# The order of small products, sums and table operations in the routing of a mixture of experts, and of its first weight load

## The reference, cut

```python
g_logits = (u @ w_group).astype(jnp.float32) + b_group          # 4 groups
p_grp, g_sel = lax.top_k(softmax(g_logits), 1)
e_logits = (u @ w_router + b_router).reshape(n, N_GROUPS, EXP_PER_GROUP)
...                                                              # the logits of the chosen group
p_exp, e_sel = lax.top_k(softmax(in_grp), TOP_E)                 # 2 experts of 8
gate = p_grp * p_exp / jnp.sum(p_exp, axis=-1, keepdims=True)
expert = g_sel * EXP_PER_GROUP + e_sel                           # 32 experts in all
...                                                              # per expert: silu(x w1) * (x w3), then w2
```

## Time and profile before

| | |
|---|---|
| median of 3 runs | 1541.97 us (1540.78 to 1544.36) |
| the profiled execution | 1542.55 us, span in the trace 1540.7 us |
| busy | PE 1386.6, DVE 719.4, ACT 527.4, POOL 211.2 us |
| transfers | 360.05 MB, mean 234 GB/s over the span |
| chain that ended last | PE 70%, DMA 18%, DVE 3%, ACT 3% |
| TensorE's granted clock, mean | 0.946 of full speed |

### The profile page before, as it was taken

The page is one execution under the profiler, slowest core; times in us unless marked ns, Lnnn a source line. Parts: engine busy times, 40 slices in busy tenths (PEclk is TensorE's granted clock), DMA queues, the critical chain, the costliest instruction groups (busy, mean ns, idle before and its releaser), DMA issues.

```text
span 1540.7 us, 27632 instructions
## 1 busy us (share of the span) xinstructions
PE 1386.6 (90%) x11864; PEld 1168.6 (76%) x11864; DVE 719.4 (47%) x1207; ACT 527.4 (34%) x815; POOL 211.2 (14%) x180
## 2 busy tenths in 40 slices
PE   6999899996777777686999989999999999999997
PEld 6998568764344444344978979999999876899997
DVE  5365665421111121113865664565456564565644
ACT  6346553110000010013334454434435434544342
POOL 4132002200000000000100023211234200111132
PEclk9999999799888798779999999999999999999999
DMA  9341218989999999999635142444454321445340
GB/s 355 139 159 54 85 56 349 393 374 428 428 429 428 428 427 429 428 428 424 238 125 208 66 178 110 163 166 150 148 199 174 141 106 60 159 176 208 126 176 28
DMA packets 32856, 360.05 MB, mean 234 GB/s; under 512 B 5376, under 2 KB 8448, under 8 KB 10752
## 3 DMA queue, kind: packets, MB, share of 16 engines
q1 hardware_dynamic: 32768, 358.76, 58.0%
HBM read 357.70 MB, written 1.05 MB: 233 GB/s over the span
## 4 chain that ended last, share of the span: by engine, by line
PE 70%; DMA 18%; DVE 3%; ACT 3%; issue 2%; SPq 1%; POOL 1%; DVEq 0%; ACTq 0%; POOLq 0%
PE PS L550 42%; DMA expert_w<-in_w 16%; PE PS L563 5%; PE PS L1013 4%; PE PS L603 3%; PE PS L1034 2%; DMA raw_x<-in_ret_qk 2%; PE PS L977 1%; SPq L400 1%; PE PS L1104 1%; PE PS L851 1%; PE PS L1189 1%; ACT wh L1443 1%; PE PS L587 1%; PE PS L579 1%
## 5 line engine op out<-in xcount | busy, mean ns | idle before, releaser
L1961 DVE TENSOR_TENSOR wl<-raw,wh 128x4096 fp32r<-128x4096 f32 (+2 forms) x66 | 267.6, 4054 | 206.8 <-ACT wh L1443 206.7
L1443 ACT ACTIVATE wh<-raw 128x4096 fp32r<-128x4096 f32 (+2 forms) x66 | 219.5, 3326 | 113.8 <-PE PS L550 108.4
L550 PE MATMUL PS<-UH,wh 128*128 128x272 f32 (+1 forms) x840 | 244.5, 291 | 11.9 <-DVE wl L2017 11.6
L550 PE MATMUL PS<-UH,wl 128*128 128x272 f32 (+1 forms) x840 | 241.4, 287 | 0.0
L550 PE MATMUL PS<-UL,wh 128*128 128x272 f32 (+1 forms) x840 | 240.9, 287 | 0.0
L1013 PE MATMUL PS<-expert_w,XW 128*32 128x256 f32 x2048 | 156.5, 461 | 86.7 <-DMA expert_w<-in_w 86.4
L1013 PEld LDWEIGHTS PS<-expert_w,XW 128*32 128x32 f32 x2048 | 70.8, 128 | 161.0 <-DMA expert_w<-in_w 106.9
L550 PEld LDWEIGHTS PS<-UH,wh 128*128 128x128 f32 x840 | 158.9, 189 | 12.9 <-DVE wl L2017 11.6
L550 PEld LDWEIGHTS PS<-UL,wh 128*128 128x128 f32 x840 | 159.3, 190 | 0.4
L550 PEld LDWEIGHTS PS<-UH,wl 128*128 128x128 f32 x840 | 159.1, 189 | 0.0
L2326 DVE TENSOR_TENSOR SG<-PS,SG 128x128 f32<-128x128 f32 x32 | 9.3, 292 | 270.0 <-ACT SG L1712 269.9
(11 more groups left out here) (526 smaller groups left out, 3025.7 us busy)
## 6 DMA issues: line engine op xcount, KB each, us to landing
expert_w<-in_w SPq DMA_DIRECT2D x96, 2048.0 KB, 20.4
raw<-in_up SPq DMA_DIRECT2D x22, 2048.0 KB, 8.2
raw<-in_down SPq DMA_DIRECT2D x16, 1408.0 KB, 6.1
raw<-in_ret_v SPq DMA_DIRECT2D x4, 2048.0 KB, 8.5
raw<-in_ret_gate SPq DMA_DIRECT2D x4, 2048.0 KB, 8.2
raw<-in_ret_o SPq DMA_DIRECT2D x4, 2048.0 KB, 8.6
raw<-in_ret_qk SPq DMA_DIRECT2D x3, 2048.0 KB, 12.9
raw<-in_w_in_ga SPq DMA_DIRECT2D x2, 2048.0 KB, 8.2
```

Source lines behind the costliest of these rows:

```text
L550: mm = pe.matmul(gbank(g)[:, c0:T], w[:, c:c + P], x(k)[:, c0:], start=(k == 0 and j == 0), stop=(k == nk - 1 and j == 2))
L1443: act.activation(WH[n % 2][:, 0:w], raw(n)[:, 0:w], ACT.Copy).then_inc(hi_done, 1)
L1961: dve.tensor_tensor(wl_of(n)[:, 0:w], raw(n)[:, 0:w], WH[n % 2][:, 0:w].bitcast(F32), ALU.subtract).then_inc(lo_done, 1)
```

## The change

Of TensorE's stream: the zero products of banks 0 and 1 move from ahead of the sums to behind them; the keep_busy counts 2, 1, 3 and 10 become 5, none, none and 4; the table's product (L967) moves behind dispatch, and the wait for the table and the load of the loop bound to behind the first hidden products. Of VectorE's: the slots are made from two terms, of which the first (the slot without overflow) and the overflow masks are formed once the ranks are there, without the prefix sums; three operations of the table move behind `window(0)`. Of ScalarE's: the wait for the table moves to its loop bound. Of SyncE's: the load of w2[1] goes ahead of the wait for `wo` and of the eight small tables.

```diff
+            sp.wait_ge(lo_done, 12)
+            load(XPT[2][:], a["w2"][1], xp_full[2])
             sp.wait_ge(unit_done, UNIT0["wo"])
             for name in ("RB", "DESC", "utri", "THR", "IOTA", "WRT", "EBASE", "SLOT"):
                 load(small[name][:], a["m_" + name], moe_in)
-            sp.wait_ge(lo_done, 12)
-            load(XPT[2][:], a["w2"][1], xp_full[2])
...
-            zeroed(0)
-            zeroed(1)
             MM, CC, CB, TA = (small[x] for x in ("MM", "CC", "CB", "TA"))
-            keep_busy(sbank(0), 2)
+            keep_busy(sbank(0), 5)
             pe.wait_ge(rt_m, 1)
...
             mm.then_inc(rank_done, 1)
-            keep_busy(sbank(0), 1)
             pe.wait_ge(rt_m, 2)
...
-            keep_busy(sbank(0), 3)
-            pe.wait_ge(rt_m, 3)
-            pe.matmul(sbank(2)[0:1, 0:OVER + 1], ones[0:NE, 0:1], TA[0:NE, 0:OVER + 1], start=True, stop=True)\
-                .then_inc(rank_done, 1)
+            zeroed(0)
+            zeroed(1)
...
-            keep_busy(sbank(0), 10)
+            keep_busy(sbank(0), 4)
             pe.wait_ge(perm_done, 2)
             pe.wait_ge(rank_free, 1)
             dispatch(True)
+            pe.wait_ge(rt_m, 3)
+            pe.matmul(sbank(2)[0:1, 0:OVER + 1], ones[0:NE, 0:1], TA[0:NE, 0:OVER + 1], start=True, stop=True)\
+                .then_inc(rank_done, 1)
...
-            pe.wait_ge(tbl_done, 1)
...
-            last = pe.value_load(TBL[0:1, ITEMS + 1:ITEMS + 2], min_val=NE - 2, max_val=ITEMS - 2)
             pe.wait_ge(xw_half, 1)
             hidden(0, 0, True)
+            pe.wait_ge(tbl_done, 1)
+            last = pe.value_load(TBL[0:1, ITEMS + 1:ITEMS + 2], min_val=NE - 2, max_val=ITEMS - 2)
             hidden(0, 1)
...
-            act.wait_ge(tbl_done, 1)
             act.nop().then_inc(xye_done, 2)
...
+            act.wait_ge(tbl_done, 1)
             last = act.value_load(TBL[0:1, ITEMS + 1:ITEMS + 2], min_val=NE - 2, max_val=ITEMS - 2)
...
-            dve.wait_ge(rank_done, 3)
-            link(dve.tensor_copy(CC[e, 2:3], sbank(1)[e, NE:NE + 1]))
-            link(dve.tensor_scalar(TA[e, 0:OVER], IO[e, 0:OVER], CC[e, 2:3], None, ALU.is_ge))
-            dve.tensor_copy(TA[e, OVER:OVER + 1], CC[e, 1:2]).then_inc(rt_m, 1)
-            link(dve.tensor_tensor(q["BK"][:], sbank(1)[:, 0:NE], EBASE[:, 1, :], ALU.add))
-            link(dve.scalar_tensor_tensor(out=CODE[:], in0=rank, scalar=float(WIN), in1=bc(q["BK"][:].unsqueeze(1), [P, NT, NE]),
-                                          op0=ALU.is_ge, op1=ALU.mult))
-            link(dve.tensor_tensor(CODE[:], CODE[:], bc(EBASE[:, 0, :].unsqueeze(1), [P, NT, NE]), ALU.add))
-            dve.tensor_tensor(CODE[:], CODE[:], rank, ALU.add).then_inc(rank_free, 1)
+            dve.wait_ge(rank_done, 2)
+            dve.tensor_tensor(CODE[:], rank, bc(EBASE[:, 0, :].unsqueeze(1), [P, NT, NE]), ALU.add)
+            for c, o in enumerate(("O1", "O2")):
+                ins = dve.scalar_tensor_tensor(out=OVR[:, c], in0=rank, scalar=float(WIN), in1=q[o][:],
+                                               op0=ALU.is_ge, op1=ALU.mult)
+            ins.then_inc(rank_free, 1)
             dve.wait_ge(rank_free, 1)
             for c, o in enumerate(("O1", "O2")):
-                link(dve.tensor_tensor(q["ET"][:], CODE[:], q[o][:], ALU.mult))
-                link(dve.tensor_reduce(DST[:, c, :], q["ET"][:], AX.X, ALU.add))
+                ins = dve.tensor_tensor(CHO[:, c], CODE[:], q[o][:], ALU.mult)
+            link(ins)
+            dve.tensor_reduce(BASE[:], CHO[:], AX.X, ALU.add)
+            dve.wait_ge(rank_done, 3)
+            link(dve.tensor_tensor(q["BK"][:], sbank(1)[:, 0:NE], EBASE[:, 1, :], ALU.add))
+            for c in range(2):
+                ins = dve.tensor_tensor(OVR[:, c], OVR[:, c], bc(q["BK"][:].unsqueeze(1), [P, NT, NE]), ALU.mult)
+            link(ins)
+            link(dve.tensor_reduce(DST[:], OVR[:], AX.X, ALU.add))
+            link(dve.tensor_tensor(DST[:], DST[:], BASE[:], ALU.add))
...
             window(0)
+            link(dve.tensor_copy(CC[e, 2:3], sbank(1)[e, NE:NE + 1]))
+            link(dve.tensor_scalar(TA[e, 0:OVER], IO[e, 0:OVER], CC[e, 2:3], None, ALU.is_ge))
+            dve.tensor_copy(TA[e, OVER:OVER + 1], CC[e, 1:2]).then_inc(rt_m, 1)
```

More of the change, by code:

```diff
@@ L243, in program @@
                         ("M1", [NT]), ("M2", [NT]), ("TM", [NT]), ("MM", [NT, 32]), ("CODE", [NT, 32]),
-                        ("BK", [32]), ("DST", [2, NT]), ("GATES", [2, NT]), ("CC", [8]), ("CB", [P]), ("N7", [7]),
+                        ("BK", [32]), ("CHO", [2, NT, 32]), ("OVR", [2, NT, 32]),
+                        ("BASE", [2, NT]), ("DST", [2, NT]), ("GATES", [2, NT]), ("CC", [8]), ("CB", [P]), ("N7", [7]),
                         ("TA", [OVER + 1]), ("TF", [ITEMS + 2]), ("EBASE", [2, NE]), ("SLOT", [1]), ("RSC", [NT]), ("ROOT", [1])]:
@@ L2256, in _ @@
             rank = sbank(3)[:, 0:NT * NE].rearrange("p (t e) -> p t e", t=NT)
-            dve.wait_ge(rank_done, 3)
-            link(dve.tensor_copy(CC[e, 2:3], sbank(1)[e, NE:NE + 1]))
-            link(dve.tensor_scalar(TA[e, 0:OVER], IO[e, 0:OVER], CC[e, 2:3], None, ALU.is_ge))
-            dve.tensor_copy(TA[e, OVER:OVER + 1], CC[e, 1:2]).then_inc(rt_m, 1)
-            link(dve.tensor_tensor(q["BK"][:], sbank(1)[:, 0:NE], EBASE[:, 1, :], ALU.add))
-            link(dve.scalar_tensor_tensor(out=CODE[:], in0=rank, scalar=float(WIN), in1=bc(q["BK"][:].unsqueeze(1), [P, NT, NE]),
-                                          op0=ALU.is_ge, op1=ALU.mult))
-            link(dve.tensor_tensor(CODE[:], CODE[:], bc(EBASE[:, 0, :].unsqueeze(1), [P, NT, NE]), ALU.add))
-            dve.tensor_tensor(CODE[:], CODE[:], rank, ALU.add).then_inc(rank_free, 1)
+            CHO, OVR, BASE = q["CHO"], q["OVR"], q["BASE"]
+            dve.wait_ge(rank_done, 2)
[4 more added lines that the diff above has]
+            ins.then_inc(rank_free, 1)
             dve.wait_ge(rank_free, 1)
             for c, o in enumerate(("O1", "O2")):
-                link(dve.tensor_tensor(q["ET"][:], CODE[:], q[o][:], ALU.mult))
-                link(dve.tensor_reduce(DST[:, c, :], q["ET"][:], AX.X, ALU.add))
+                ins = dve.tensor_tensor(CHO[:, c], CODE[:], q[o][:], ALU.mult)
[8 more added lines that the diff above has]
+            link(dve.tensor_tensor(DST[:], DST[:], BASE[:], ALU.add))
             def window(pair):
```

## The result

The changed kernel took 1544.73 us, the median of 20 runs (1541.92 to 1548.22); the kernel before, run beside it, 1542.03 (20 runs, 1537.89 to 1544.55). The ratio is 1.0023, 95% interval [1.0015, 1.003]: 2.7 us slower on the medians, clear of no change by the interval, but under the 3.1 us that the prediction set as its bound for "slower". The profiled execution took 1544.41 (span 1542.6) against 1542.55 (span 1540.7).

The account below looks back on a forecast made before the run. One saturated stream of expert loads bounds the kernel, its start set by xh_done 4. Dispatch's end +1.85, hidden +2.0 and loop bound +0.4 give +4.2 on 1542.55, less 0.6: 1546.2 us; range 1538.6 to 1549.2, likeliest case 1543.7 to 1549.5.

Parts of the forecast that it names:

- the later stretch: Half-clock stretch from 296, behind zero products 2 and 3: stays in another alignment, up to 1.5 us either way.
- Rival C: Dispatch at half clock, but hidden products recover at once or the stretch behind 296 is 2 us kinder: about 1544.2; chance 0.10.
- Step 1: First expert load ahead of the small tables: first batch ends 0 to 4.9 us earlier, worth 0.
- rival D: The early load matters, not routing: the batch's earlier end pulls the next loads; 1542.0, chance 0.05.
- Step 2: TensorE up to the sums: sums start at 267.4 instead of 269.0, prefix sums done at 270.1 instead of 272.29.
- Step 3: VectorE's new order: PERM done at 272.6 instead of 275.62, 3.0 us earlier.
- Step 4: TensorE from sums to dispatch: zero products 3.71 us at half clock, then keep_busy; dispatch at 275.8 instead of 277.14, -1.3.
- Step 5: Dispatch at half clock: its 32 products take 6.85 us, +3.3; dispatch ends 1.85 us later.
- Step 6: Hidden products of items 0 and 1 run partly at half clock: +2.0 us, between +1 and +3.
- Step 7: Load of the loop bound, moved between the two hidden products: 0.4 us uncovered (0 to 0.85).
- rival B: Busy is busy: clock up from the first five rounds or through the zero products, dispatch at 273.1; 1538.3, chance 0.14.
- Rival A: Clock rises in keep_busy ahead of dispatch, zero products still at half clock: -0.9 us, 1541.1; chance 0.13.

Follow-up runs that it names:

- with all rows: The changed kernel with all four zero products on 128 rows of zeros instead of one: 1536.84 us, ratio 0.9958 to the kernel before.
- the kernel with ten rounds: The changed kernel with ten keep_busy rounds instead of four ahead of dispatch: 1541.58 us, ratio 0.9994 to the kernel before.
- the last version: The changed kernel with 128-row zero products, one group ahead of the sums with seven keep_busy rounds, one behind with six: 1536.26 us, ratio 0.996.

## Why the prediction was right, point by point

The forecast was 1546.2 us and the median is 1544.73, inside the range and in the likeliest case's own. The mechanism held: dispatch and the hidden products ran at half clock, and the experiments tie the loss to that. That the number came so near is in part luck. Terms of the sum and the later stretch came out 3 us smaller than forecast (+1.2 us at xh_done 4, counted from the routing's start, instead of +4.2), and a half-clock stretch at the last item, which the prediction didn't have, added 1.7. Most of the chance (0.57) had gone to a time above 1545.05, which was not reached. Rival C (about 1544.2) is as near; of its two alternatives the first failed (the hidden products did not recover at once) and the second, a later stretch kinder by 2 us, came out at 1.6.

- **The bound (one saturated stream from xh_done 4 on): held.** From 400 to 500 us after shows the same as the earlier trace rows; behind the second batch the engines are idle from 319.0 to 320.5, and the load goes out at 319.55. That load came 0.30 us later than in before and the last item's 0.25 later, one for one; with all rows, where the stream has no hole left, 9.9 us became 8.2. The two windows:

```profile
319.00:320.00 1.00, 0.75 (x10) 0.30 (x2) 0.29 (x1) 0.60 (x2) 0.00 (x0) 1.00 0.00 0
...
400.00:500.00 100.00, 72.43 (x900) 42.91 (x892) 16.58 (x57) 7.42 (x23) 0.00 (x0) 0.88 1.01 428
```

- **Step 1 (early load, 0): held.** The batch ended at 282.3 and the engines then stood idle until 287.6; the next load was issued at 286.71. The hole only got longer. This is also against rival D.
- **Step 2 (sums at 267.4): held** at 266.34 + 0.9 = 267.2. **Step 3 (VectorE): the order held, the size was low.** PERM 4.2 us earlier instead of 3.0, for the most part since the sums ran at full clock and ended at 268.31 + 0.9 = 269.2 instead of 270.1.
- **Step 4 (zero products 3.71 at half clock, then dispatch at 275.8): right in kind, mis-sized by 1.1.** The zero products started at 268.31 + 0.9 = 269.2, not 270.2, because the clock was up from 264.6 to 268.0. I had ruled a rise out there ("the 1.15 us of it before the sums brought no rise"), reading the effect of five rounds from that of two. Dispatch started at 273.82 + 0.9 = 274.7.
- **Step 5 (dispatch at half clock, 6.85): held**, 6.72 in the chain. The 0.213 us for one product doesn't follow from the two rows, which give 0.23 (4.55 us for the 20 left behind the fall); 0.210 was measured. **Step 6 (hidden +2.0): held**, 9.06 - 7.11 = +1.95; the clock came back 4.0 us into the stage.
- **Step 7 (loop bound uncovered, 0.4): wrong, 0.** The 128 products run as one piece of 9.06 us, without a stall in the middle. Between dispatch and them lie 0.3 us, as many as before.
- **The sum at the end of hidden: +4.2 forecast, +2.8 measured**, of which 1.1 is step 4 and 0.4 step 7. **The later stretch: "up to 1.5 either way", came out at -1.6.** Relative to routing's start xh_done 4 was thus only 1.2 us late (319.55 + 0.9 against 319.25), and in the span 0.3. (The forecast's spread, added up from its terms, would run from 1543.3 to 1549.2, not from 1543.7 to 1549.5; nothing hangs on it.)
- **What I did not have: the last item.** The profiled executions differ by 1.9, and only 0.3 of it is the stream. TensorE's timeline of before and of after, at the last item's hidden products:

```profile
714.59 1.93 PE L1013 MATMUL PS<-expert_w,XW 128*32 128x256 f32 x32 [1.50 <-DMA expert_w<-in_w]
```

```profile
714.84 3.64 PE L1010 MATMUL PS<-expert_w,XW 128*32 128x256 f32 x32 [1.26 <-DMA expert_w<-in_w]
```

The load lands 0.25 later, but these 32 products run at half clock in after and at full in before: +1.71. Nothing behind them hides it: in ten of the twelve traces the span ends 824.1 to 824.4 us after the last item's hidden products do (822.9 and 823.0 in the two with the load undone). So the 1.9 us between the profiled executions are 0.25 of stream and 1.7 of clock at the last item. That second part isn't tied to the change: with all rows these products took 1.93 in three of the traces and 3.64 in two. So one execution of each kernel can't say how often it comes, and how much of the 2.7 us between the medians it makes stays open. The same goes for the spread of 6 us among the runs of each kernel: the traces show two things that can make it, the last item (1.7 us) and the moment at which the routing begins (259.8 to 263.3 under the same code), and not in what shares.

The rule of the Trainium skill on keeping TensorE busy ("TensorE: Matmul & The Clock Gate", "Why this matters for your kernels") was rival B's, at 14%. The trace disagrees: the engine is busy from 268 to 285, but for 0.16 us, at a granted clock of 0.50, and the clock returns at 271.7 when the four zero-product instructions ahead of dispatch use 128 rows in place of one.

Rival A's time came with more filler: that is the kernel with ten rounds (1541.58, forecast for A 1541.1), though the clock rose inside dispatch there and not ahead of it. Four rounds, about half of the 3.6 us of filler that lay ahead of the rise in before, weren't enough, as stated against it.

## What to carry to other kernels

Read the granted clock beside every stretch of filler and bookkeeping on TensorE, and before moving such a stretch next to critical products ask what shape its products have: a busy engine is not a clocked one. A product that serves only to clear a bank cost no more on all rows than on one at the same clock, and with all rows the clock came back ahead of or in the first products of dispatch; that one-line edit took 7.9 us off the changed kernel, where the whole reordering had cost 2.7. An engine's freed microseconds count only if the other engine is there to take them: here PERM came 4.2 us earlier and waited for 3.3.

## What the runs showed of the hardware

- Two zero products (four instructions) of 1 row x 512 columns took 1.91 us at full clock and 3.71 at half; on 128 rows 1.72 and 3.71 (3.58 where the clock rose near their end).
- The clock was lost behind one-row zero products every time that they ran at full clock: at 272.8 with the load undone, and behind zero products 2 and 3 in all six kernels that have them on one row, 0.1 to 2.5 us behind their end (296.3 in before, 298.7 in after, 295.1 with ten rounds). Behind zero products 2 and 3 on 128 rows it was lost in none of six. Where the first two zero products on 128 rows stand behind the sums, the clock was back 2.9, 3.3 (271.7 - 268.40) and 5.4 us behind their start in three traces; ahead of the sums, 1.5 us behind it (264.5 - 262.99), as early as with keep_busy in that place (264.6 in after). They don't keep it by themselves in every place: in both after and the version with all rows it fell at 268.0 to 268.3, as the zero products began, behind the sums (1 to 32 columns, 1.19 us of idle time ahead of them), and in the last version at 266.6, in the sums, 2.2 us behind filler that followed a 128-row product.
- Dispatch's products (128x64 each), 32 of them without a gap, didn't bring the clock back: 6.72 us at 0.50. From the first keep_busy product ahead of dispatch to the rise passed 13 us in after (272.0 to 285.0), 12.6 in the kernel with TensorE's half alone (276.9 to 289.5), 6.1 with ten rounds (271.9 to 278.0) and 3.6 in before. What in the products between makes this difference stays open; no run varied dispatch's columns alone.
- Dispatch's 32 products took 0.110 us each at full clock and 0.210 at half (3.52 and 6.72): the same factor as for products of 256 columns (1.93 and 3.64 for 32).
